# Weights of v for two chunks at a time, the high part on ScalarE; h in rows of 512 tokens for each k; gates and spilled gelus laid out in DRAM by fours of chunks

## The reference, cut to what matters

```python
def peer_ffn(h, wq, sub_keys, u, v):
    ...
        q = jnp.einsum('td,de->te', xc, wq).reshape(PEER_CHUNK, PEER_HEADS, 2, PEER_QDIM // 2)
        s = jnp.einsum('thpd,hpnd->thpn', q, sub_keys).astype(jnp.float32)
        sv, si = lax.top_k(s, PEER_TOPK)
        ...
        eidx = jnp.take_along_axis(cidx, pos, axis=-1)
        g = jax.nn.softmax(top, axis=-1)
        ue = u[eidx]
        ve = v[eidx]
        a = jax.nn.gelu(jnp.einsum('thkd,td->thk', ue, xc).astype(jnp.float32), approximate=False)
        return jnp.einsum('thk,thkd->td', (g * a).astype(ve.dtype), ve)
```

## Time and profile before

| what | us |
|---|---|
| three runs: median (lowest to highest) | 1567.95 (1567.89 to 1569.85) |
| span of the profiled execution | 1565.4 |
| PE busy in it | 1527.4 (98%) |
| PEld busy | 1363.9 (87%) |
| DVE busy | 1337.7 (85%) |
| ACT busy | 660.1 (42%) |
| POOL busy | 487.5 (31%) |
| DMA packets under 2 KB / all | 75369 / 160467 |

### The profile page before, as it was taken

How to read it: one execution, slowest core, us unless ns; L and a number is a source line. 1 busy time by engine, 2 the same in 40 slices (tenths; PEclk the granted TensorE clock), 3 DMA queues, 4 the chain that set the end, 5 groups by cost and what they waited for, 6 DMA issues and landing times.

```text
span 1565.4 us, 24588 instructions
## 1 busy us (share of the span) xinstructions
PE 1527.4 (98%) x8275; PEld 1363.9 (87%) x8275; DVE 1337.7 (85%) x2877; ACT 660.1 (42%) x1143; POOL 487.5 (31%) x450
## 2 busy tenths in 40 slices
PE   4999999999999999999999999999999999999997
PEld 4887767888999999999999999999999998888886
DVE  5788666549999989899698898899999998999977
ACT  3444554233344757657433333343333332333232
POOL 1121300033450000020355455456566663233000
PEclk9999999999999999999999999999999999999999
DMA  9754410132355565676899999999999999999772
GB/s 366 270 174 148 148 68 0 55 95 82 118 169 180 194 230 199 229 248 251 298 393 330 350 340 343 346 337 371 372 378 372 368 345 355 376 350 352 241 244 104
DMA packets 160467, 398.77 MB, mean 255 GB/s; under 512 B 11753, under 2 KB 75369, under 8 KB 158705
## 3 DMA queue, kind: packets, MB, share of 16 engines
q1 hardware_dynamic: 112992, 227.06, 41.7%
q0 software_dynamic: 36864, 134.23, 23.2%
q10 hardware_dynamic: 10514, 36.30, 5.9%
HBM read 359.27 MB, written 38.27 MB: 254 GB/s over the span
## 4 chain that ended last, share of the span: by engine, by line
PE 83%; DVE 13%; DMA 1%; ACT 1%; issue 1%; ACTq 0%; DVEq 0%; SPq 0%
PE bank_S L907 16%; PE bank_T L907 11%; PE bank_O L858 6%; PE bank_O L856 6%; PE bank_O L857 6%; PE bank_T L885 5%; PE bank_G L907 5%; PE bank_S L856 3%; PE bank_S L857 3%; PE bank_S L858 3%; PE bank_O L643 2%; PE bank_S L610 2%; DVE mod_acc L1909 1%; DVE v_sb L1902 1%; DVE v_sb L1915 1%; DVE si L1921 1%
## 5 line engine op out<-in xcount | busy, mean ns | idle before, releaser
L1462 ACT ACTIVATE v_hi<-v_raw 128x1024 fp32r<-128x1024 f32 x124 | 131.7, 1062 | 333.9 <-PE bank_G L907 330.9
L1434 ACT ACTIVATE u_hi<-u_raw 128x1024 fp32r<-128x1024 f32 x128 | 135.9, 1061 | 243.0 <-PE bank_O L858 122.8
L1213 POOL COPY stage<-eidx 128x1 uint32<-128x1 uint32 (+1 forms) x128 | 75.7, 591 | 461.8 <-DVE eidx L2030 207.7
L1217 POOL DMA_INDIRECT row<-in_peer_u,stage x128 | 148.1, 1157 | 103.8 <-POOL stage L1213 103.8
L856 PE MATMUL bank_S<-h_hi,u_hi 128*128 128x384 f32 x512 | 179.7, 351 | 0.5 <-DVE u_lo L2002 0.5
L858 PE MATMUL bank_O<-h_hi,u_lo 128*128 128x384 f32 x512 | 171.9, 336 | 0.0
L856 PE MATMUL bank_O<-h_hi,u_hi 128*128 128x384 f32 x512 | 171.7, 335 | 0.0
L858 PE MATMUL bank_S<-h_hi,u_lo 128*128 128x384 f32 x512 | 171.5, 335 | 0.0
L857 PE MATMUL bank_O<-h_lo,u_hi 128*128 128x384 f32 x512 | 171.5, 335 | 0.0
L857 PE MATMUL bank_S<-h_lo,u_hi 128*128 128x384 f32 x512 | 171.4, 335 | 0.0
L2098 DVE SCALAR_TENSOR_TENSOR y<-row,wgt,y 128x1024 f32<-128x1024 f32 x128 | 165.9, 1296 | 0.0
(11 more groups left out here) (370 smaller groups left out, 3647.8 us busy)
## 6 DMA issues: line engine op xcount, KB each, us to landing
u_raw<-in_u_t SPq DMA_DIRECT2D x128, 512.0 KB
v_raw<-in_peer_v SPq DMA_DIRECT2D x128, 512.0 KB
gates<-g_out ACTq DMA_DIRECT2D x12, 2048.0 KB, 6.8
g_in<-gates SPq DMA_DIRECT2D x32, 768.0 KB
ada_late<-in_w_ada SPq DMA_DIRECT2D x8, 2048.0 KB, 8.4
spill<-a_act ACTq DMA_DIRECT2D x56, 192.0 KB, 2.1
a_act<-spill SPq DMA_DIRECT2D x14, 768.0 KB, 10.6
w_raw<-in_w_in SPq DMA_DIRECT2D x20, 512.0 KB, 4.1
```

The costliest lines, as they stand in the source:

```text
L1217: pool.indirect_dma_start(rows[slot][:, :], None, table[:, :], bass.IndirectOffsetOnAxis(stage[:, place:place + 1], 0))\
L1434: act.activation(u_hi[c % 2][:, :], u_raw[:, c % 2, :], ACT.Copy).then_inc(s_uhi, 1)
L1462: act.activation(v_hi_end[:, i % TAIL, :] if end else v_hi[:, c % 2, :], v_raw[c % 4][:, :], ACT.Copy)\
```

## The change

**Layout of h.** `h_hi` and `h_lo` become [k][512 tokens] instead of [tile][k][128 tokens]. The moving operand of a matmul, three or four pieces of 128 columns before, is one run. The columns of tile 0 are not needed by the dense part; `y0` and the second buffer of `u_lo` now lie in them, as 8 pieces of 128, and so do two high parts of w_out while the last tile's columns are still empty. `junk` goes: the row dots write over the gathered row. The space freed takes a double buffer of weights for pairs of chunks.

**Weights in pairs.** `product` (DVE) multiplies gelus and gates of two chunks in place in `g_in`, `w_high` (ACT, new) copies the pair to its high part, `w_low` (DVE) subtracts. `w_low` stands at the head of an even chunk on DVE, `product` of the next pair at the head of an odd one, `w_high` at the end of an even chunk on ACT. `w_f` goes. The gates' load waits for `w_low` instead of the product.

**Layout in DRAM.** `gates` is [partition][four of chunks][token block][chunk of four][32 tokens], so that a load of four chunks is one run of 6 KB for a partition and a store of a token block is 32 runs of 512 B for a partition. Before it was the other way round: a load of 12 runs of 512 B, a store of one run of 16 KB. `spill` keeps 1536 B runs for the store, and a load becomes one run of 6 KB for a partition, 4 runs of 1536 B before.

The diff, cut to its core (the helpers `by_k`, `half_columns`, `weight_pair` only make views; two buffers' addresses and w_out's views are left out):

```diff
@@ -159,8 +159,8 @@
...
-        h_hi = at("h_hi", 32, [P, NT, KD, P], f32r)
-        h_lo = at("h_lo", 64, [P, NT, KD, P], f32r)
+        h_hi = at("h_hi", 32, [P, KD, S], f32r)
+        h_lo = at("h_lo", 64, [P, KD, S], f32r)
@@ -175,30 +175,28 @@
...
-        y0 = at("y0", 32, [P, D])
-        g_in = at("g_in", 56, [P, 2, DT // GB, 4, GB])
+        y0 = at("y0", 32, [P, KD, S])[:, :, 0:P]
+        g_in = [at(f"g_in{j}", kib, [P, DT // GB, 4, GB]) for j, kib in enumerate((56, 182))]
...
-        u_lo = [at(f"u_lo{j}", kib, [P, D], f32r) for j, kib in enumerate((92, 84))]
+        u_lo = [at("u_lo0", 92, [P, KD, P], f32r)[:, :, :], h_lo[:, :, 0:P]]
...
-        w_f = at("w_f", 128, [P, DT])
-        w_hi = at("w_hi", 130, [P, 2, DT], f32r)
-        w_lo = at("w_lo", 133, [P, 2, DT], f32r)
-        rows = [at(f"row{j}", k, [P, D]) for j, k in enumerate((104, 108, 136, 168, 176, 184,
-                                                                     140, 144, 148, 152, 156, 160))]
-        junk = at("junk", 180, [P, D])
+        w_hi = [at(f"w_hi{j}", kib, [P, 2, DT], f32r) for j, kib in enumerate((128, 194))]
+        w_lo = [at(f"w_lo{j}", kib, [P, 2, DT], f32r) for j, kib in enumerate((176, 179))]
+        rows = [at(f"row{j}", k, [P, D]) for j, k in enumerate((84, 104, 108, 136, 160, 168,
+                                                                     132, 140, 144, 148, 152, 156))]
...
+        w_lo_end = at("w_lo_end", 132, [P, TAIL, DT], f32r)
@@ -293,8 +291,8 @@
...
-        gates = nc.dram_tensor("gates", [DT // GB, P, NCHUNK, GB], f32).ap()
-        spill = nc.dram_tensor("spill", [SPILL, P, DT], f32).ap()
+        gates = nc.dram_tensor("gates", [P, NCHUNK // 4, DT // GB, 4, GB], f32).ap()
+        spill = nc.dram_tensor("spill", [SPILL // 4, P, 4, DT], f32).ap()
@@ -306,6 +304,28 @@
...
+        def half_columns(h, i, half):
+            return h[:, 4 * half:4 * half + 4, i * P:i * P + P]
+        def by_k(row):
+            return row.rearrange("p (k c) -> p k c", k=KD)
+        def gate_pair(c):
+            return g_in[c // 4 % 2][:, :, c % 4:c % 4 + 2, :].rearrange("p b i t -> p i b t")
+        def by_block(pair):
+            return pair.rearrange("p i (b t) -> p i b t", t=GB)
+        def weight_pair(w, w_end, i, c):
+            if at_end(i):
+                q = i % TAIL
+                return by_block(w_end[:, q:q + 2, :])
+            return by_block(w[c // 2 % 2][:, :, :])
@@ -853,9 +882,9 @@
...
-                    pe.matmul(ps[:, 0:DT], u_hi[q][:, kk], h_hi[:, GT:NT, k, :], start=(k == 0), stop=False)
-                    pe.matmul(ps[:, 0:DT], u_hi[q][:, kk], h_lo[:, GT:NT, k, :], start=False, stop=False)
-                    mm = pe.matmul(ps[:, 0:DT], u_lo[q][:, kk], h_hi[:, GT:NT, k, :], start=False, stop=(k == KD - 1))
+                    pe.matmul(ps[:, 0:DT], u_hi[q][:, kk], h_hi[:, k, GT * P:S], start=(k == 0), stop=False)
+                    pe.matmul(ps[:, 0:DT], u_hi[q][:, kk], h_lo[:, k, GT * P:S], start=False, stop=False)
+                    mm = pe.matmul(ps[:, 0:DT], u_lo[q][:, k, :], h_hi[:, k, GT * P:S], start=False, stop=(k == KD - 1))
@@ -896,15 +925,16 @@
...
-                pe.wait_ge(s_w, i + 1)
+                pe.wait_ge(s_w, over(i, c, 2) + 1)
...
-                q = c % 2
+                q, pair = c % 2, c // 2 % 2
...
-                            mm = pe.matmul(y_bank[t][half][:, :], w[:, q, tt], v[:, q, half * 512:half * 512 + 512],
+                            mm = pe.matmul(y_bank[t][half][:, :], w[pair][:, q, tt],
+                                           v[:, q, half * 512:half * 512 + 512],
@@ -1088,13 +1118,14 @@
...
-                    after(sp, s_pw, 4 * (q - 1))
-                    sp.dma_start(g_in[:, parity, :, :, :].rearrange("p b i t -> p b (i t)"),
-                                 gates[:, :, bass.ds(chunk_of(4 * q, late), 4), :].rearrange("b p i t -> p b (i t)"))\
+                    after(sp, s_w, 2 * (q - 1))
+                    own = q - MAIN // 4 if late or (isinstance(q, int) and 4 * q >= MAIN) else q + SPILL // 4
+                    sp.dma_start(g_in[parity][:, :, :, :].rearrange("p b i t -> p (b i t)"),
+                                 gates[:, bass.ds(own, 1), :, :, :].rearrange("p o b i t -> p (o b i t)"))\
...
-                                     spill[bass.ds(q * 4 - MAIN, 4)].rearrange("i p t -> p i t"))\
+                                     spill[bass.ds(q - MAIN // 4, 1)].rearrange("o p i t -> p (o i) t"))\
@@ -1196,8 +1227,10 @@
...
+                if i == 1:
+                    taken(pool, ("q", 2 * PH - 1))
...
-                pool.tensor_tensor(u_lo[c % 2][:, :], u_raw[:, c % 2, :], u_hi[c % 2][:, :].bitcast(f32),
+                pool.tensor_tensor(u_lo[c % 2], by_k(u_raw[:, c % 2, :]), by_k(u_hi[c % 2][:, :]).bitcast(f32),
@@ -1462,6 +1494,17 @@
...
+            def w_high(i, c):
+                if not within(i):
+                    return
+                if at_end(i):
+                    act.wait_ge(s_acc, PH * TOPK)
+                else:
+                    after(act, s_yv, i - 2)
+                act.wait_ge(s_pw, over(i, c, 2) + 1)
+                act.activation(weight_pair(w_hi, w_hi_end, i, c), gate_pair(c), ACT.Copy).then_inc(s_whi, 1)
@@ -1480,7 +1523,7 @@
...
-                act.dma_start(spill[i], a_act[:, i % AHEAD, :]).then_inc(s_as[i % 2], 16)
+                act.dma_start(spill[i // 4, :, i % 4, :], a_act[:, i % AHEAD, :]).then_inc(s_as[i % 2], 16)
@@ -1509,8 +1552,8 @@
...
-                    act.dma_start(gates[tb].rearrange("p i t -> p (i t)"),
-                                  g_out[tb % 2][:, :, :].rearrange("p i t -> p (i t)")).then_inc(s_gst[tb % 2], 16)
+                    act.dma_start(gates[:, :, tb, :, :].rearrange("p q i t -> p q (i t)"),
+                                  g_out[tb % 2][:, :, :].rearrange("p (q i) t -> p q (i t)", i=4)).then_inc(s_gst[tb % 2], 16)
@@ -1521,6 +1564,8 @@
...
+            w_high(0, 0)
@@ -1534,14 +1579,16 @@
...
-                        act.wait_ge(s_pw, m + 1)
+                        act.wait_ge(s_pw, over(m, c, 2) + 1)
...
+                if c % 2 == 0:
+                    w_high(m + 2, c + 2)
...
-                act.activation(rows[0][:, part], x_sb[:, i, part], ACT.Square, accum_out=to).then_inc(s_f2, 1)
+                act.activation(rows[2][:, part], x_sb[:, i, part], ACT.Square, accum_out=to).then_inc(s_f2, 1)
@@ -2063,30 +2107,30 @@
...
-            done(dve, dve.memset(y0[:, :], 0.0), s_dv)
+            done(dve, dve.memset(y0, 0.0), s_dv)
...
-            def weigh(i, c, late):
-                dve.wait_ge(s_g[(c // 4) % 2], 16 * (over(i, c, 8) + 1))
+            def product(i, c):
+                if not within(i):
+                    return
+                late = isinstance(i, int) and i >= MAIN
+                dve.wait_ge(s_g[c // 4 % 2], 16 * (over(i, c, 8) + 1))
...
-                    dve.wait_ge(s_al[c // 4], 2 * (i - c) - 2 * MAIN + 16)
+                    dve.wait_ge(s_al[c // 4 % 2], 16 * ((i - MAIN) // AHEAD + 1))
...
-                    dve.wait_ge(s_gelu, i + SPILL + 1)
-                dve.tensor_tensor(w_f[:, :].rearrange("p (b t) -> p b t", t=GB),
-                                  a_act[:, c, :].rearrange("p (b t) -> p b t", t=GB),
-                                  g_in[:, (c // 4) % 2, :, c % 4, :], ALU.mult).then_inc(s_pw, 1)
-                dve.wait_ge(s_pw, i + 1)
-                end = at_end(i)
-                hi, lo = (w_hi_end, w_lo_end) if end else (w_hi, w_lo)
-                q = i % TAIL if end else c % 2
-                if not end:
-                    after(dve, s_yv, i - 1)
-                dve.tensor_copy(hi[:, q, :], w_f[:, :]).then_inc(s_whi, 1)
-                dve.wait_ge(s_whi, i + 1)
-                dve.tensor_tensor(lo[:, q, :], w_f[:, :], hi[:, q, :].bitcast(f32), ALU.subtract)\
-                   .then_inc(s_w, 1)
-                dve.wait_ge(s_w, i + 1)
+                    dve.wait_ge(s_gelu, i + SPILL + 2)
+                slot = c % AHEAD
+                dve.tensor_tensor(gate_pair(c), by_block(a_act[:, slot:slot + 2, :]), gate_pair(c), ALU.mult)\
+                   .then_inc(s_pw, 1)
+            def w_low(i, c):
+                dve.wait_ge(s_whi, over(i, c, 2) + 1)
+                if not at_end(i):
+                    after(dve, s_yv, i - 2)
+                dve.tensor_tensor(weight_pair(w_lo, w_lo_end, i, c), gate_pair(c),
+                                  weight_pair(w_hi, w_hi_end, i, c).bitcast(f32), ALU.subtract).then_inc(s_w, 1)
@@ -2109,7 +2153,10 @@
...
-                weigh(i, c, late)
+                if c % 2 == 0:
+                    w_low(i, c)
+                else:
+                    product(i + 1, c + 1)
@@ -2118,7 +2165,8 @@
...
-                    dve.scalar_tensor_tensor(out=junk[:, :], in0=rows[2 * place][:, :], scalar=1.0, in1=h2[:, 0, :],
```

(35 more changed lines are left out.)

10 lines of the change are left out of this document (3 added, 7 removed).

## The result

The changed kernel takes 1616.83 us (median, 1615.64 to 1618.32) against 1568.24 us (1567.89 to 1569.85) of the kernel before, taken beside it. The ratio is 1.031, with a 95% interval of 1.0296 to 1.0325. The change costs 48.6 us. The forecast was 1600.0 us within 1569 to 1613: slower, as forecast, but by half as much again, and outside the range. The profiled execution's span is 1614.2 us, 1565.4 before.

A forecast was written before the change was run, and what follows sets the result against it. PE was taken as the bound from 768 us on, and in the gate stage with little to spare. Terms of 27.2 + 4.4 = 31.6 us on 1567.95 gave 1599.6, say 1600 us; range 1569 to 1613.

The forecast's parts named there:

- h in rows of 512 tokens: Matmuls reading h as one run gain 0; POOL's u splits written in pieces, bounded by 10%, stay hidden: 0.
- the rival "faster": Where u and v alternate, one run of h removes 0.08 us in 63 chunks, 5 us: 1563; chance 0.05.
- Weights in pairs: In the loop, DVE is relieved of 67 us and ACT takes 64 copies, neither awaited by PE: 0.
- Start of the loop: First weight up to 1.2 us later plus handovers, offset by a lighter gates load; bounds 0 and 1.5 us, taken 0.
- Loads of gates and gelus: SP's 32 loads drop from 1536 packets to 128; nothing in the loop waits for them on PE: 0.
- The issue behind a store: Gate stage: the spilled gelu's issue after a gate store holds ACT; PE stands 3.4 us in 8 blocks, 27.2 us.
- the limit of 85: A queue's next issue waits until about 85 packets for each engine are left; bounded by 57 and 113.
- u behind a store: After each tile's last block, u waits behind a store 2 us longer; PE loses 4.4 us in three places.
- The clock: The forecast sum added no time for a slower clock; 14 us for it stood only in a rival.
- ACT's queue takes the store whole: The store's own issue grows slightly and the next is not held: 1573.8 us; chance 0.22.
- The clock falls too: PE's stalls each followed by as long at half speed, 14 us on top: 1614; chance 0.13 with blocked store.
- Nothing is late: Small packets let u pass and the issue is free: 1566 to 1571 us, likeliest 1568; chance 0.17.

The follow-up runs named there:

- the kernel with PE kept busy: The changed kernel with 15 matmuls whose result nobody reads on PE ahead of the third group in eight blocks; 1603.97 us, ratio 1.0228.

## Why the prediction was right or wrong

*h in rows of 512 tokens: 0.* Right. POOL's splits of u, one written in one run and the next in pieces of 128 (start, us):

```profile
411.88 2.40 POOL L1233 TENSOR_TENSOR u_lo<-u_raw,u_hi 128x1024 fp32r<-128x1024 f32 x1 [3.09 <-ACT u_hi L1466]
416.04 2.39 POOL L1233 TENSOR_TENSOR h_lo<-u_raw,u_hi 128x1024 fp32r<-128x1024 f32 x1 [1.76 <-ACT u_hi L1466]
```

2.39 and 2.40 us, so the bound of 10% was not touched. VectorE's took 1225 ns in pieces and 1218 in one run. The other way round too: the chunks in which u and v alternate keep their 8.31 us, and where u is alone, up to 508 us, both kernels reach the end within 0.1 us of each other, so the rival "faster" falls.

*Weights in pairs: 0.* Right, and so were the prices, estimated as 0.95, 0.8 and 0.95 us (groups of the whole span, shapes apart; busy us, mean ns):

```profile
L2124 DVE TENSOR_TENSOR g_in<-a_act,g_in 128x768 f32<-128x768 f32 x64 | 60.8, 951 | 0.0
L2132 DVE TENSOR_TENSOR w_lo<-g_in,w_hi 128x768 fp32r<-128x768 f32 x62 | 59.0, 952 | 1.0 <-ACT w_hi L1506 1.0
L1506 ACT ACTIVATE w_hi<-g_in 128x768 fp32r<-128x768 f32 x62 | 51.7, 833 | 1.0 <-DVE g_in L2124 0.9
```

*Start of the loop: 0, bounds 0 and 1.5.* 0.3 us on PE. *Loads of gates and gelus: 0.* Right, by the spacing of 8.31 and 4.08 us.

*The issue behind a store: 27.2 us.* The mechanism, the place, the eight blocks and, in most blocks, the limit of 85 are as forecast. The size was 30.9 us of waits, 3.86 us each instead of 3.4, since two figures of the time line were short: the first packet came 1.2 us after the store's issue began, not 0.9 (the issue itself grew from 0.34 to 0.54 us), and a packet took 28.6 ns (2751 of them in 4.92 us of 16 engines), not 27.6. 1.2 + 171 x 28.6 ns = 6.1 us instead of 5.6. It lies within the bounds of 21 and 33.

*u behind a store: 4.4 us.* Too much. ACT waited 4.50 us for u after the last block (3.73 before, 5.7 by the forecast), so the wait did not grow by the 2 us of the forecast. From 798.70 to 802.60 us only ACT's queue moved packets (packets, MB, share of 16 engines), though u's load had been issued at 798.33:

```profile
q10 hardware_dynamic: 2293, 1.17, 107.2%
```

But u's first packet came at 802.70 us, with 61 packets of the store for each engine still left, and not after its end; that is 4.37 us after the issue, 4.46 before. After the other two blocks ACT waited 2.33 and 2.60 us, where the held spill had delayed ACT itself: the two delays overlap there, and I had added them. PE lost about 1.9 us in the three places by its starts. As to the rule of the Trainium skill ("DMA: Bandwidth & Descriptors", Queues, rings and completion order) by which u would pass a store of small packets: here u stood while 143 packets of the store for each engine went ahead of it, and loads of u issued with nothing else on the way usually began after 0.96 us. The small packets did not let u pass unhindered. Whether u's packets were ready in that time the trace doesn't show.

*The clock: 0 in the sum.* This is the step that failed. The prediction saw the clock at 0.50 in the earlier trace rows and priced its fall at 14 us, as a rival of 0.13 together with another one, but summed the likeliest case at full clock. I had no reason for that: eight stands of 3.4 us on an engine otherwise always busy were my own forecast, and a row showed the lower level in a stretch in which PE was idle 2.8 us of 10.2. The fall was 12.9 us by the kernel with PE kept busy, whose 1603.97 us is what the sum of 1600 described. A stand of PE of this length has two prices, and I counted one. The range failed with it: its upper end, 1613, lay below the 1614 that the text itself had worked out for this case.

The sum by what was measured, with the stands by PE's starts: 32.2 + 1.9 + 0.3 + 12.9 = 47.3 of 48.6 us. 1.3 us are not assigned; the runs of one kernel lie 2 to 3 us apart.

*The rivals.* "ACT's queue takes the store whole" fell with the rows of 4 us: 256 packets for each DMA engine cost ACT 0.2 us in their own issue and 3.7 in the next one. "The clock falls too" is what happened: 12.9 us where it had 14. "Nothing is late" fell with the result.

## What to carry to other kernels

The packets of a DMA are not only its own cost: before one is cut finer, look at what its engine issues next in the same queue, count the packets for each DMA engine that will be left by then, and ask who stands behind that issue; cut the DMA into parts under the limit (128 packets for each engine were free in most blocks here, 64 in nearly all), or give the next one another queue. When a forecast has PE standing still for some microseconds again and again, put the lower clock after each stand into the sum, not among the rivals. A layout that makes a load that nobody waits for cheap and a store that somebody stands behind dear is a loss whatever the totals say.
